# Two ways to sum over partitions in the modulation of a two-block DiT kernel

## The reference

```python
def ada_params(cvec, w, b):
    m = jax.nn.silu(cvec) @ w + b
    return jnp.split(m[..., None, :], N_MOD, axis=-1)
```

## Time and profile before

| what | value |
|---|---|
| median of 3 runs | 4533.46 us (4528.8 to 4538.09) |
| profiled execution | 4533.59 us, its span 4531.8 us |
| TensorE (PE) busy | 3894.3 us, 86% |
| VectorE (DVE) busy | 2909.9 us, 64% |
| ScalarE (ACT) / GpSimd (POOL) busy | 1924.4 us / 884.6 us |
| slab sums on VectorE (L375) | 392 instructions, 319.2 us |
| one-column products (L387) | 448 records, 61.7 us |
| AttentionIn, first FfnIn, HyenaIn | about 116 to 248, 509 to 772, 1030 to 1178 us |

### The profile page before, as it was taken

One profiled execution on the slowest core, in us unless ns is written; L12 is line 12 of the kernel. 1 busy time (PEld: TensorE's weight loads), 2 busy tenths in 40 slices (PEclk: granted clock), 3 DMA queues, 4 the chain that ended last, 5 costly groups with the idle time before them and its releaser, 6 DMA issues. The chain is left out here.

```text
span 4531.8 us, 52259 instructions
## 1 busy us (share of the span) xinstructions
PE 3894.3 (86%) x18812; PEld 3122.0 (69%) x18812; DVE 2909.9 (64%) x3455; ACT 1924.4 (42%) x2311; POOL 884.6 (20%) x460
## 2 busy tenths in 40 slices
PE   4889899969988989588888888689999695999995
PEld 3756577727566777488888887468888473788883
DVE  6754776378658763345455445479998443899994
ACT  2132432223023322433333333267777222777773
POOL 0300000003100000022222221135554001454550
PEclk9989999979998999699999999889999897999997
DMA  5420354305413441000000001199998312999992
GB/s 185 153 95 19 109 170 167 108 28 206 156 38 112 167 158 38 18 19 19 19 19 19 19 19 38 37 338 362 356 368 301 132 56 88 391 368 365 365 356 104
DMA packets 372880, 689.31 MB, mean 152 GB/s; under 512 B 38867, under 2 KB 118867, under 8 KB 372116
## 3 DMA queue, kind: packets, MB, share of 16 engines
q1 hardware_dynamic: 327696, 639.79, 39.8%
q10 hardware_dynamic: 25764, 30.93, 2.0%
q0 software_dynamic: 19296, 16.94, 1.1%
HBM read 697.95 MB, written 41.00 MB: 163 GB/s over the span
## 5 line engine op out<-in xcount | busy, mean ns | idle before, releaser
L565 PE MATMUL psum<-work_rounded 128*128 128x512 f32 x3504 | 1163.9, 402 | 98.3 <-DVE work_rounded L559 31.1
L559 DVE TENSOR_TENSOR ring_rounded<-ring,work_rounded 128x2048 fp32r<-128x2048 f32 (+1 forms) x445 | 816.0, 1836 | 410.3 <-ACT work_rounded L554 281.3
L565 PEld LDWEIGHTS psum<-work_rounded 128*128 128x128 f32 x3504 | 668.2, 192 | 267.7 <-issue 117.4
L565 PE MATMUL psum<-work_rounded,fixed_rounded 128*128 128x512 f32 x2544 | 784.5, 403 | 26.8 <-DVE fixed_rounded L559 7.3
L565 PE MATMUL psum<-work_rounded,ring_rounded 128*128 128x512 f32 (+1 forms) x1824 | 725.2, 398 | 0.0
L554 ACT ACTIVATE work_rounded<-ring 128x1024 fp32r<-128x1024 f32 x204 | 214.6, 1057 | 989.2 <-PE psum L565 690.7
L2992 ACT ACTIVATE work_rounded<-ring 128x2048 fp32r<-128x2048 f32 x256 | 490.8, 1919 | 261.3 <-PE psum L565 175.7
L565 PEld LDWEIGHTS psum<-work_rounded,fixed_rounded 128*128 128x128 f32 x2544 | 484.6, 190 | 146.3 <-issue 15.5
L565 PE MATMUL psum<-fixed_rounded,work_rounded 128*128 128x512 f32 (+1 forms) x1088 | 431.4, 396 | 0.0
L565 PEld LDWEIGHTS psum<-work_rounded,ring_rounded 128*128 128x128 f32 x1824 | 350.3, 192 | 79.2
L559 DVE TENSOR_TENSOR work_rounded<-work,work_rounded 128x2048 fp32r<-128x2048 f32 (+1 forms) x196 | 337.6, 1733 | 41.9 <-ACT work_rounded L2992 37.5
(11 more groups left out here) (329 smaller groups left out, 5878.7 us busy)
## 6 DMA issues: line engine op xcount, KB each, us to landing
ring<-in_w SPq DMA_DIRECT2D x128, 2048.0 KB, 13.2
work<-in_w SPq DMA_DIRECT2D x64, 2048.0 KB, 13.0
ring<-in_mod_w SPq DMA_DIRECT2D x24, 2048.0 KB, 8.4
ring<-in_ada_w SPq DMA_DIRECT2D x24, 2048.0 KB, 8.0
ring<-in_ffn_w_in SPq DMA_DIRECT2D x44, 1024.0 KB, 7.6
ring<-in_ffn_w_out SPq DMA_DIRECT2D x10, 2048.0 KB, 7.9
ring<-in_w_in_a SPq DMA_DIRECT2D x32, 512.0 KB, 6.3
ring<-in_hy_w_in SPq DMA_DIRECT2D x6, 2048.0 KB, 7.9
```

The costliest lines, as they stand in the source:

```text
L559: return eng.tensor_tensor(c.rounded(v), v, c.rounded(v_high), ALU.subtract)
L565: ins = pe.matmul(out, c.rounded(w), c.rounded(x), start=(start and i == 0), stop=(stop and i == 2))
```

## The change

`Modulation` gets a second way to sum over partitions, used where an accumulator was passed and there is no context condition (`wide`): in AttentionIn, the first FfnIn and HyenaIn, 8 + 12 + 12 = 32 of the 56 sums. TensorE makes one product, 128 x 128 ones stationary and the accumulator (128 x 512) moving, into the whole of bank 7: each row then holds the 512 sums. VectorE, in the new `collect`, multiplies this by the identity, repeated four times, into the accumulator, and reduces each 128 columns to one, which leaves the sum of column p in row p. `collect(s - 1)` is called at the start of `vector_slab` s, and for the last slab in `finish`. The product of the next sum waits for the semaphore `mod_taken` of the collect before it.

```diff
--- before.py
+++ after.py
@@ -338,6 +338,7 @@
         super().__init__(core)
         self.layer, self.bias, self.w = layer, bias, w
         self.acc = W0 if acc is None else acc
+        self.wide = acc is not None and cond_ctx is None
 
         self.first, self.slabs = slabs[0], slabs[1] - slabs[0]
 
@@ -348,6 +349,8 @@
                 self.add_slab()
         self.summed, self.base = core.shared("mod_summed", self.before(self.slabs))
         self.turned, _ = core.shared("mod_turned", self.before(self.slabs))
+        if self.wide:
+            self.taken, self.taken0 = core.shared("mod_taken", self.before(self.slabs))
 
     def add_slab(self):
         s = self.first + len(self.n)
@@ -359,6 +362,8 @@
 
     def vector_slab(self, dve, s):
         c = self.c
+        if self.wide and s:
+            self.collect(dve, s - 1)
         w = c.slot(self.n[s], KD, 512)
         c.arrived(dve, self.n[s])
         q = self.before(s)
@@ -378,11 +383,29 @@
                     ins.then_inc(self.summed, 1)
         c.used(dve.drain(), self.n[s])
 
+    def collect(self, dve, s):
+
+        c = self.c
+        q = self.before(s)
+        ident = c.const("ident").unsqueeze(1).to_broadcast([P, 4, P])
+        for i, (_, col) in enumerate(self.jobs[s]):
+            own = c.view(self.acc + 512 * ((q + i) % 4), 4, P)
+            dve.wait_ge(self.turned, self.base + q + i + 1)
+            dve.tensor_tensor(own, c.ps[:, 7, :].rearrange("p (a n) -> p a n", a=4), ident, ALU.mult)
+            dve.drain()
+            dve.tensor_reduce(c.view(ADA0 + 64 * self.layer + col, 4), own, AX.X, ALU.add).then_inc(self.taken, 1)
+
     def tensor_slab(self, pe, s):
         c = self.c
         q = self.before(s)
         for i, (_, col) in enumerate(self.jobs[s]):
             pe.wait_ge(self.summed, self.base + q + i + 1)
+            if self.wide:
+                if q + i:
+                    pe.wait_ge(self.taken, self.taken0 + q + i)
+                pe.matmul(c.ps[:, 7, :], c.const("ones"), c.view(self.acc + 512 * ((q + i) % 4), 512),
+                          start=True, stop=True).then_inc(self.turned, 1)
+                continue
             for j in range(4):
                 ins = pe.matmul(c.ps[:, 7, col + j:col + j + 1], c.view(self.acc + 512 * ((q + i) % 4) + 128 * j, P),
                                 c.const("ones")[:, 0:1], start=True, stop=True)
@@ -391,13 +414,19 @@
     def finish(self, dve):
 
         c = self.c
-        dve.wait_ge(self.turned, self.base + self.before(self.slabs))
         out = c.view(ADA0 + 64 * self.layer, 64)
         a, b = 4 * self.first, 4 * (self.first + self.slabs)
-        dve.tensor_tensor(out[:, a:b], c.ps[:, 7, a:b], c.pars(self.bias)[:, a:b], ALU.add)
         contexts = len(self.jobs[0]) == 2
+        if self.wide:
+            self.collect(dve, self.slabs - 1)
+            dve.drain()
+            src = out
+        else:
+            dve.wait_ge(self.turned, self.base + self.before(self.slabs))
+            src = c.ps[:, 7, :]
+        dve.tensor_tensor(out[:, a:b], src[:, a:b], c.pars(self.bias)[:, a:b], ALU.add)
         if contexts:
-            dve.tensor_tensor(out[:, 48:64], c.ps[:, 7, 48:64], c.pars(self.bias)[:, 0:16], ALU.add)
+            dve.tensor_tensor(out[:, 48:64], src[:, 48:64], c.pars(self.bias)[:, 0:16], ALU.add)
         dve.drain()
         for what in (1, 4) + ((7,) if contexts else ()):
             if what == 7 or a <= 8 * what < b:
```

## The result

The changed kernel takes 4653.93 us (median of 4 runs, 4650.52 to 4660.9) against 4532.79 us (four runs of the kernel before, one more than shown above): a ratio of 1.0268, 95% interval 1.0251 to 1.0286, 121 us slower. The profiled execution took 4654.91 us with a span of 4653.1 us.

What follows compares the result with a forecast made beforehand. TensorE carries the three stages and VectorE has slack, so new waits decide: AttentionIn 12, FfnIn 20, HyenaIn 84, less 5 given back, make +111 us on 4533.6, forecast 4645 us, range 4610 to 4688.

Steps and rivals of the forecast that it cites:

- TensorE's part: All 32 changed sums: one wide product takes about as long as four one-column products; at most 1 us, left out.
- A collect: VectorE's product, drain and reduction for each changed sum: 1.4 us together, bounds 1.1 and 1.8.
- AttentionIn: 12: Serial chain of products, collects and slabs at the stage's end +10.7, an earlier slab wait +1.4: 12 us.
- FfnIn: 20: First FfnIn: TensorE stalls before tile 7 (+9.8) and after product 10 (+5.9), collect delays, slow clock 1.5: 20 us.
- HyenaIn: 84: Four 13.6 us weight-load stalls (53 net), slow clock 6, two smaller waits 10, longer stage end 15: 84 us.
- two smaller waits: HyenaIn: ScalarE waiting for convolutions at tiles 10 to 15, VectorE's long rounds in tiles 8 to 15: together 10 us.
- Collisions: VectorE against GpSimd in HyenaIn: collects keep their length, nothing added; 11 us in all if they were hit.
- Given back: HyenaConv's 8.2 us table wait shrinks as one slab loads before the barrier: -5 us, bounds 0 and -8.
- work without stalls: Rival: only VectorE's extra time counts, loads come soon enough and only stage ends grow: +37, 4571 us; 6%.
- A worse HyenaIn: Rival: longer slow clock, loads of 10 to 13 us, ScalarE's wait each round: +40 on top, 4685 us; 9%.
- Not slower: Rival: TensorE takes the wide product in one pass, saving 14 us in all: 4520 us; 1%.
- It doesn't do what it says: Rival: `wide` is false everywhere, so nothing changes; 1%.

Runs made afterwards that it cites:

- kernel 1: The kernel before, with only VectorE's wait for TensorE's product of sum s-1 ahead of slab s added, no wide product or collect: 4631.94 us, ratio 1.0218.
- kernel 2: The changed kernel with the same products and collects, each collect placed where TensorE's product is already done: 4564.03 us, ratio 1.0063 to before.
- 3: The changed kernel with HyenaIn's weight slab k in the ring slot of sum slab 2k-3 instead of 2k-2: 4609.39 us, ratio 1.0165 to before.
- 5: The kernel before with slab 11 of both FfnIn moved behind tile 40's convolution and product 11 to the end: 4524.80 us, ratio 0.9976.
- kernel 7: Wide product and collects in HyenaIn alone, AttentionIn and FfnIn as in the kernel before: 4617.15 us, ratio 1.0178 to before.
- 6: The changed kernel with FfnIn's product 0 issued after tile 2 instead of tile 6: 4636.03 us, ratio 1.0218 to before.
- 4: Kernel 2 with product and reduction of each collect done twice: 4592.77 us, ratio 1.0124 to before.

## Why the prediction was right

Forecast 4645 us, +111; measured 4654, +121, inside the range. The mechanism is shown: the named signs are there (in HyenaIn VectorE waits five times 15 to 17 us for the wide product and ScalarE 15 to 23 us for each of four weight slabs), and kernels 1 to 3 take wait, work and ring slot apart. That HyenaIn came out to within 1 us is in part luck. The 10 us missing are 4 in FfnIn, 4 that were not given back, and 2 between and behind the stages, where the forecast had nothing (4.7 lost, 2.8 won besides what was given back). By its steps:

- **TensorE's part: nothing.** Five pairs of neighbouring side products in HyenaIn (0 and 1, 2 and 3, to 8 and 9) have two unstalled tiles between them; they lie 12.1 us apart, as before. Right.
- **A collect: 1.4 us.** 687 and 686 ns, from 1114.99 to the slab behind it (1116.34) 1.4 us. Right; the reduction is nearer 0.7 than 0.64.
- **AttentionIn: 12, measured 12.8.** Product 5 to `finish` takes 21.3 us (239.46 to 260.71) where 20.3 were forecast. The missing microsecond is the last wide product: after its 7.7 us wait it runs at the 1.2 GHz level and lasts 2.08 instead of 1.02 us.

```profile
239.46 1.02 PE L406 MATMUL psum<-work,fixed 128*128 128x512 f32 x2
...
257.06 2.08 PE L406 MATMUL psum<-work,fixed 128*128 128x512 f32 x2 [7.72 <-DVE work L380]
```

- **FfnIn: 20, measured 24.** Both predicted stalls are there; TensorE's timeline, changed kernel:

```profile
556.40 1.02 PE L406 MATMUL psum<-work,fixed 128*128 128x512 f32 x2
565.14 2.08 PE L406 MATMUL psum<-work,fixed 128*128 128x512 f32 x2 [7.72 <-DVE work L380]
568.08 0.77 PE L594 MATMUL psum<-work_rounded 128*128 128x512 f32 x1 [0.86 <-DVE ring_rounded L588]
...
763.42 0.40 PE L594 MATMUL psum<-work_rounded,ring_rounded 128*128 128x512 f32 x1
766.54 0.77 PE L594 MATMUL psum<-work_rounded 128*128 128x512 f32 x1 [2.72 <-DVE ring_rounded L588]
...
786.13 1.02 PE L406 MATMUL psum<-work,fixed 128*128 128x512 f32 x2
794.87 2.08 PE L406 MATMUL psum<-work,fixed 128*128 128x512 f32 x2 [7.72 <-DVE work L380]
797.80 0.76 PE L594 MATMUL psum<-work_rounded 128*128 128x512 f32 x1 [0.86 <-DVE ring_rounded L588]
```

  Product 0 to tile 7 takes 11.7 us, product 10 to tile 43 11.7 us (forecast 11.5 each). What was too small is the step "collect 8 delays the slot that the last weight slab waits for by 1.4": the pause ahead of tile 40 did grow by 1.5 us, to 3.1, and then the three tiles to product 10 took 19.6 us (766.54 to 786.13) instead of 16.7. The first 14 distances between the product starts of tile 40 are 0.43 us or more, the 1.2 GHz level, and soon 0.23 behind them; in the kernel before, behind a pause of 1.6 us, they are 0.23 from the second on.
- **HyenaIn: 84, measured 83.2, with errors that cancel.** The four stalls are 14.6, 14.5, 12.8 (in two parts) and 16.0 us, 58 in place of 54: the load took 8.0 us for 7.8, and VectorE came to the collect 2.0 to 3.7 us behind the product instead of 1.1. The tile behind each took 7.0 to 7.6 us instead of 5.6, on average 1.8 more instead of 1.5. Against that, the 10 us for "two smaller waits" did not add. ScalarE's wait for a convolution is in the trace and made TensorE wait 3.0 us ahead of tile 15, but that tile lies between product 5 and tile 16, a stretch whose length (21.3 us, 1194.41 to 1215.69) is set by collect, slab and load as in the other turns (21.2); the stall ahead of tile 16 came out shorter instead (9.8). Ahead of product 0, where the forecast had nothing, 2.3 us were added: the load for tile 4 took 0.8 us longer, and behind the resulting pause of 3.5 us the tile took 7.3 us. In total product 0 to product 9 takes 176.4 us (1100.67 to 1277.10), 64.7 more than the 111.7 of before; forecast was 69. The end is 25.2 us (1277.10 to 1302.28), 16.2 more than the 9.0 of the earlier trace rows, forecast 15. 2.3 + 64.7 + 16.2 = 83.2.
- **Collisions: nothing added.** Right for the collects, which keep their 0.69 us in HyenaIn too, but the term was not nothing. The slab sum's first instruction, a scalar product with one SBUF input, took 0.48 us in all twelve slabs of the kernel before; now it takes 1.19 in five and 0.86 in one, where GpSimd was at work (here from 1102.01 to 1104.01):

```profile
1101.73 0.69 DVE L394 TENSOR_TENSOR work<-psum,fixed 128x512 f32<-128x512 f32 x1 [17.28 <-PE psum L406]
1102.50 0.69 DVE L396 TENSOR_REDUCE fixed<-work 128x4 f32<-128x512 f32 x1
1103.10 1.19 DVE L376 TENSOR_SCALAR work<-ring,fixed 128x512 f32<-128x512 f32 x1
1104.36 7.52 DVE L380 SCALAR_TENSOR_TENSOR work<-ring,fixed,work 128x512 f32<-128x512 f32 x7
```

  The Trainium skill (SBUF — State Buffer, Who interferes with whom) counts `tensor_scalar` among the instructions that can take the port shared with GpSimd; the row agrees. Slab 1 took 8.9 us here instead of 6.4 (1103.10 to the convolution at 1112.01; GpSimd worked again from 1108.51), which is why VectorE came to collect 1 at 1114.99, 2.2 us behind product 1.
- **Given back: 5.** HyenaConv's wait for its table fell from 8.2 to 5.0 us, right in kind, but the whole stretch from HyenaIn's biases to the next stage's first slab sum is only 0.7 us shorter (208.3 instead of 209.0). The term was too large by 4; what took up the rest was not followed. The wait that is left:

```profile
  DMA fixed<-in_hy_back: 5.0, 1
```

Of the rivals, "work without stalls" (+37) falls by kernel 1, which has the stalls without the work; what remains in kernel 2, +31, is near its price of 37, though in part by another way (TensorE's wait for the single bank). "A worse HyenaIn" has one of its signs (slow tiles) but neither loads of 10 us and more nor its size. "Not slower" never applied: the wide product costs TensorE what the four narrow ones did. "It doesn't do what it says" falls by the 32 collects in the trace.

## What to carry to other kernels

When a step that ran on one engine gets a second half on another, look at where both engines' lists have it, not only at what it costs: here 44 us of hidden-looking work cost 31 us, 11 of them by a wait of TensorE for the single bank, and its place in the list 90 more. Follow what the waiting instruction holds behind it, queue by queue; the dearest item was a ring slot, freed so late that TensorE stood idle for 13 to 16 us, four times, until its load was there. And a small product that one engine makes several tiles after its input can be collected only several tiles later still.

## What the runs showed that I had not expected

- A pause of TensorE of about 3 us already costs more than itself: ahead of tile 40 in FfnIn 1.5 us more pause gave 2.9 us more for the three tiles behind it. The Trainium skill (TensorE: Matmul & The Clock Gate, Why this matters for your kernels) warns of such gaps, and these rows agree; what one costs here, beside itself, is 1.3 to 2.9 us for pauses of 2.7 to 16 us, and it does not grow with their length (2.9 behind the shortest, 1.3 behind the longest).
- Time is lost in stretches without a changed instruction too. From the biases of AttentionIn to FfnIn's first sum 263.8 us pass instead of 261.6. In the 38 us that begin 14.5 us after those biases TensorE's mean granted clock is 0.74 instead of 0.90. Over the nine kernels clock and length go together: 0.86 to 0.90 with 261.2 to 261.6 us (before, 1, 2 and 5), 0.77 with 262.5 and 263.3 (7 and 6), 0.74 with 263.8 and 263.9 (changed, 3 and 4). That the clock is the cause was not tried, and kernel 7, which has the instructions of the kernel before up to there, shows 0.9 us of it as well.
